# Mixtures of experts: rows gathered as quarters and transposed by VectorE, in place of whole rows and TensorE's transposes

## What is computed

```python
def hier_moe(x, norm_g, w_rg, w_re, w_gate, w_up, w_down):
    u = rms_norm(x, norm_g)
    lg = jnp.einsum('ntd,dg->ntg', u, w_rg)                 # 4 groups
    p_top, g_sel = lax.top_k(jax.nn.softmax(lg), 1)         # one group
    ...
    top_v, top_i = lax.top_k(le, TOP_K)                     # two of its 4 experts
    ...
    h = jax.nn.silu(jnp.einsum('ntd,edf->ntef', u, w_gate)) * jnp.einsum('ntd,edf->ntef', u, w_up)
    h = h * dense_w[..., None]
    return jnp.einsum('ntef,efd->ntd', h, w_down)
```

## Time and profile before

| | |
|---|---|
| median of 3 runs | 1412.71 us (1411.58 to 1415.81) |
| the profiled execution | 1418.34 us, its span 1416.5 us |
| TensorE busy | 1312.3 us, 93% of the span, mean granted clock 0.943 |
| VectorE, ScalarE, GpSimd busy | 38%, 21%, 12% |
| DMA | 437.02 MB, 309 GB/s mean; about 390 GB/s in the mixtures |

### The profile page before, as it was taken

How to read it: one execution, slowest core, us unless ns; L and a number is a source line. 1 busy time by engine, 2 the same in 40 slices (tenths; PEclk the granted TensorE clock), 3 DMA queues, 4 the chain that set the end, 5 groups by cost and what they waited for, 6 DMA issues and landing times.

```text
span 1416.5 us, 36477 instructions
## 1 busy us (share of the span) xinstructions
PE 1312.3 (93%) x15444; PEld 1004.0 (71%) x15444; DVE 540.7 (38%) x1274; ACT 297.5 (21%) x715; POOL 168.4 (12%) x202
## 2 busy tenths in 40 slices
PE   6979999999897989999989999999999799999996
PEld 5869999998535767666755655655546799999983
DVE  3740000000375647564756676664025200000005
ACT  2201111111231131313234343434110111111110
POOL 3110000010201111121211111120000100000003
PEclk9979999999997999999989899898998899999998
DMA  8959999998998699999978797974373599999976
GB/s 284 374 194 354 388 390 390 390 389 340 341 357 273 199 330 335 300 358 301 358 245 299 240 335 236 344 250 169 117 282 134 201 380 385 390 389 391 392 305 208
DMA packets 147223, 437.02 MB, mean 309 GB/s; under 512 B 20711, under 2 KB 51304, under 8 KB 138270
## 3 DMA queue, kind: packets, MB, share of 16 engines
q1 hardware_dynamic: 99494, 367.57, 70.1%
q10 hardware_dynamic: 37296, 38.09, 8.4%
q0 software_dynamic: 10320, 29.79, 6.7%
HBM read 406.31 MB, written 29.44 MB: 308 GB/s over the span
## 4 chain that ended last, share of the span: by engine, by line
PE 65%; issue 12%; DVE 9%; DMA 6%; ACT 3%; SPq 3%; ACTq 1%; POOL 1%; DVEq 0%; POOLq 0%
PE PS L1098 12%; PE PS L1102 11%; PE PS L1351 9%; PE PS L1130 6%; PE PS L1135 5%; PE PS L1485 5%; PE PS L1020 3%; PE PS L1391 2%; PE PS L1429 2%; PE PS L1437 2%; PE PS L1449 2%; SPq L680 1%; DMA W<-in_cache_v 1%; DVE KV L2425 1%; DMA KV<-in_cache_k 1%
## 5 line engine op out<-in xcount | busy, mean ns | idle before, releaser
L1102 PE MATMUL PS<-W,KV 128*32 128x128 f32 x3072 | 344.2, 274 | 0.0
L1098 PE MATMUL PS<-W,KV 128*32 128x384 f32 x3072 | 340.9, 490 | 3.2 <-DVE KV L2046 3.2
L1102 PEld LDWEIGHTS PS<-W,KV 128*32 128x32 f32 x3072 | 336.9, 111 | 1.9
L2286 DVE TENSOR_TENSOR KV<-KV,PS 128x384 f32<-128x384 f32 x32 | 17.7, 554 | 481.5 <-PE PS L1116 426.7
L1351 PE MATMUL PS<-W 128*128 128x256 f32 x768 | 178.2, 386 | 1.3 <-ACT KV L1758 1.3
L1351 PEld LDWEIGHTS PS<-W 128*128 128x128 f32 x768 | 144.2, 193 | 30.8 <-issue 8.8
L1130 PE MATMUL PS<-W,KV 128*32 128x384 f32 x1440 | 162.2, 489 | 0.0
L1135 PE MATMUL PS<-W,KV 128*32 128x256 f32 x960 | 162.2, 327 | 0.0
L2425 DVE STREAM_TRANSPOSE KV<-KV 128x1024 f32<-128x1024 f32 x128 | 154.9, 1226 | 7.8 <-DMA KV<-in_cache_k 7.7
L1098 PEld LDWEIGHTS PS<-W,KV 128*32 128x32 f32 x3072 | 150.5, 109 | 4.5 <-DVE KV L2046 4.1
L1135 PEld LDWEIGHTS PS<-W,KV 128*32 128x32 f32 x960 | 95.6, 109 | 14.4
(11 more groups left out here) (306 smaller groups left out, 1512.4 us busy)
## 6 DMA issues: line engine op xcount, KB each, us to landing
W<-in_w_gate SPq DMA_DIRECT2D x32, 2048.0 KB, 14.4
W<-in_w_up SPq DMA_DIRECT2D x32, 2048.0 KB, 15.5
W<-in_w_down SPq DMA_DIRECT2D x32, 2048.0 KB, 14.4
KV<-in_cache_k SPq DMA_DIRECT2D x256, 256.0 KB, 5.4
W<-in_cache_v SPq DMA_DIRECT2D x128, 512.0 KB, 7.7
yd<-KV ACTq DMA_DIRECT2D x30, 288.0 KB, 7.8
W<-in_w_kvf SPq DMA_DIRECT2D x4, 2048.0 KB, 18.2
W<-in_w_kvf ACTq DMA_DIRECT2D x8, 1024.0 KB, 8.6
```

Source lines behind the costliest of these rows:

```text
L1098: pe.matmul(PS[32 * q:32 * q + 32, bank, 0:WIDE], x, w[:, k, 0:WIDE], start=(k == 0), stop=(k == KC - 1), tile_position=(0, 32 * q), skip_ ...
L1102: mm = pe.matmul(PS[CAP:P, bank, P * q:P * q + P], x, w[:, k, WIDE:FF], start=(k == 0 and q == 0), stop=(k == KC - 1), tile_position=(0, C ...
```

## The change

A gathered row becomes four quarters of 256 features: XS is seen as `XS4`, in which row r is rows 4r to 4r + 3. XS is written with its features in another order (`in_quarters`), so that block transposes of 32x32 of a gathered tile give what the products need. Partition 32a + i of gather q holds quarter a of the expert's row 32q + i; three gathers of 128 quarters (1 KB each) make an expert. IDX is then a table of 3 columns for each expert, with 4 * row + a, written by 12 instructions in place of one. VectorE transposes the tile (one instruction) and multiplies it with the gains (three), into XQ[j], of which there are two, one in V4. TensorE's `x_tr` is gone; `up` gets a wait for `h_ready`, which `xt_ready` implied before.

```diff
@@ gather
-                        after(pool, sem("xt_tr"), e - 1 + l * NE)
+                        after(pool, sem("xg_read"), e - 1 + l * NE)
                         settled(pool)
-                        pool.indirect_dma_start(out=XG[j][0:CAP, :], out_offset=None, in_=XS,
-                                                in_offset=bass.IndirectOffsetOnAxis(ap=IDX[0:CAP, e:e + 1], axis=0))\
-                            .then_inc(sem(f"xg_in_{j}"), 16)
+                        for q in range(Q4):
+                            pool.indirect_dma_start(out=XG[j][:, 2 * P * q:2 * P * q + 2 * P], out_offset=None, in_=XS4,
+                                                    in_offset=bass.IndirectOffsetOnAxis(ap=IDX[:, Q4 * e + q:Q4 * e + q + 1], axis=0))\
+                                .then_inc(sem(f"xg_in_{j}"), 16)
@@ TensorE
-                def x_tr(e, j):
...
-                    transposes(XG[j], 0, CAP, KC).then_inc(sem("xt_tr"), 1)
...
-                            x = XT[:, k, 32 * q:32 * q + 32]
+                            x = XTQ[j][:, q, k, :]
...
                     else:
-                        product(3, 3 * j + 1, count, "up")
+                        after(pe, sem("h_ready"), e + l * NE)
+                        product(3, 3 * j + 1, count, "up", j)
...
                     if not first:
                         h_tr(e - 1)
-                    x_tr(e + 1, 1 - j)
-                    if not first:
                         down(e - 1, 1 - j)
...
-                x_tr(0, 0)
                 expert(0, 0)
@@ VectorE
+            def in_quarters(t, out):
+
+                r = ROWS[t]
+                return dve.tensor_scalar(out[0:r, :].rearrange("p (a k n) -> p a k n", a=4, k=KC),
+                                         H[0:r, t, :].rearrange("p (a n k) -> p a k n", a=4, k=KC), rs[0:r, t:t + 1], None, ALU.mult)
...
-                dve.tensor_copy(IDX[:, :], PS[:, 7, 2 * P:2 * P + NE]).then_inc(sem("routed"), 1)
+                table = IDX[:, :].rearrange("p (e q) -> p q e", q=Q4)
+                for q in range(Q4):
+                    for a in range(4):
+                        ins = dve.tensor_scalar(table[32 * a:32 * a + 32, q], PS[32 * q:32 * q + 32, 7, 2 * P:2 * P + NE], 4.0, float(a),
+                                                ALU.mult, ALU.add)
+                ins.then_inc(sem("routed"), 1)
...
-                def xt(e):
-                    dve.wait_ge(sem("xt_tr"), e + 1 + l * NE)
-                    gained(XT, 0, l, CAP).then_inc(sem("xt_ready"), 1)
+                def xt(e, j):
+                    dve.wait_ge(sem(f"xg_in_{j}"), 24 * e + 48 - 24 * j + l * (24 * NE))
+                    after(dve, sem("up_done"), e - 1 + l * NE)
+                    dve.transpose(XQ[j], XG[j][:, 0:Q4 * 2 * P]).then_inc(sem("xg_read"), 1)
+                    dve.wait_ge(sem("xg_read"), e + 1 + l * NE)
+                    x = XQ[j].rearrange("p (q k n) -> p q k n", q=Q4, k=KC)
+                    for q in range(Q4):
+                        g = gains[:, l, :].rearrange("p (k a) -> p k a", a=1).to_broadcast([P, KC, 32])
+                        ins = dve.tensor_tensor(x[:, q], x[:, q], g, ALU.mult)
+                    ins.then_inc(sem("xt_ready"), 1)
...
-                xt(0)
+                xt(0, 0)
+                xt(1, 1)
                 gates(l)
                 hidden(0)
-                xt(1)
+                xt(2, 0)
...
-                with dve.Fori(1, NE - 1) as e:
-                    hidden(e)
-                    xt(e + 1)
+                with dve.Fori(1, NE - 3, 2) as e:
+                    for j in range(2):
+                        hidden(e + j)
+                        xt(e + j + 2, 1 - j)
```

More of the change, by code:

```diff
@@ L340, in build @@
         SGi = sb("SGi", [P, 2, NT], I32)
[L341 to L342 removed]
+        IDX = sb("IDX", [P, NE * Q4], I32)
+        idc = sb("idc", [P, 2 * Q4], I32)
         npi = sb("npi", [1, 1], I32)
@@ L375, in build @@
         XT = V8[:, 4, :].rearrange("p (k n) -> p k n", k=KC)
+        XQ = [a[:, 0:Q4 * 2 * P] for a in (V8[:, 4, :], V4[:, :])]
+        XTQ = [a.rearrange("p (q k n) -> p q k n", q=Q4, k=KC) for a in XQ]
         SG = V8[:, 5, 0:FF]
@@ L1084, in moe, with product @@
             def moe(l):
-                def x_tr(e, j):
-                    k = 8 * e + 16 - 8 * j
-                    pe.wait_ge(sem(f"xg_in_{j}"), k + l * (8 * NE))
-                    after(pe, sem("xt_ready"), e + l * NE)
-                    transposes(XG[j], 0, CAP, KC).then_inc(sem("xt_tr"), 1)
-                def product(bank, slot, count, name):
+                def product(bank, slot, count, name, j):
                     pe.wait_ge(sem(f"w_in_{slot}"), count + l * (8 * NE))
@@ L1145, in halves @@
                         after(pe, sem("silu_done"), e + l * NE)
-                        product(2, 3 * j, count, "gate")
+                        product(2, 3 * j, count, "gate", j)
                     else:
-                        product(3, 3 * j + 1, count, "up")
+                        after(pe, sem("h_ready"), e + l * NE)
+                        product(3, 3 * j + 1, count, "up", j)
                 def expert(e, j):
@@ L1203, in moe @@
                             pe.wait_ge(sem(f"g_xg{l}"), 16 * (n + 1))
-                            transposes(XG[0], 0, P, KC).then_inc(sem(f"g_step{l}"), 1)
+                            for k in range(KC):
+                                for a in range(4):
+                                    at = 2 * P * a + 32 * k
+                                    mm = pe.matmul(PS[32 * a:32 * a + 32, k // 4, (k % 4) * P:(k % 4) * P + P], XG[0][:, at:at + 32], ident,
+                                                   start=True, stop=True, tile_position=(0, 32 * a), skip_group_check=True)
+                            mm.then_inc(sem(f"g_step{l}"), 1)
                             pe.wait_ge(sem(f"g_step{l}"), 9 * n + 2)
@@ L2024, in norm @@
                 norm_scale(phase, t)
+                if phase in ("r0", "r1"):
+                    return in_quarters(t, out)
                 if gain is None:
```

20 lines of the change are left out of this document (12 added, 8 removed).

## The result

The changed kernel takes 1434.51 us (median of 4 runs, 1432.71 to 1437.8), the kernel before 1413.78 (4 runs): the ratio is 1.0171, with a 95% interval of 1.0141 to 1.0202. It is slower by 1.7%, where I forecast 1408. The profiled span is 1436.0 us, 19.5 more than before.

What follows compares the result with a forecast made beforehand. TensorE was taken to set the pace, running on prefetched weights. The terms -11.5 - 3.2 - 1.0 + 2.0 + 5.2 + 1.3 + 2.5 gave -4.7 us, from 1412.7 to 1408.0 us, range 1400 to 1418.

Steps and rivals of the forecast that it cites:

- Part 1: TensorE between h_tr and down: each x_tr removed saves 0.41 us, not 1.06; 28 places, -11.5 us.
- Costed at nothing: In the loop, VectorE's 2.2 us and three gathers' 3.9 us of GpSimd for an expert lie beside TensorE; no cost.
- the weights come late: Rival: in the loops, smaller gather packets load the DMA and weight loads delay TensorE; 1423 at 86 ns a packet; chance 0.18.
- the DMA's own pace: Weight loads in the loop: the DMA wants about 18.2 us for an expert, TensorE 17.62, running on prefetched weights.
- Part 2: Between experts 0 and 1, x_tr(1) and its gains go from the path: 1.6 us in each layer, -3.2 us.
- the half clock: At gate(0), without x_tr, 1.3 more slow us in each layer, half lost: +1.3 us, bounds 0 and 2.7.
- Part 3: Mixture start, table to gate(0): table +2.0, gathers +5.2, VectorE's transposes and gains -1.0, slow clock +1.3 us.
- Part 4: Scalings that write rows in another order: +0.5 us for each of five on the path, +2.5 us (0 to 5).
- strided reads are slow: Rival: scalings at the skill's price for strided sources, or twice the upper bound; total 1415; chance 0.14.

Runs made afterwards that it cites:

- e5: The changed kernel with each expert's three gathers put apart, the later two behind the signals for down and gate, table used in place: 1416.94 us, ratio 1.004.
- e14: As e13, with the table given to GpSimd in three parts, so the first gather is issued after four of twelve instructions: 1384.13 us, ratio 0.9806.
- e13: The changed kernel with h_tr(e - 1) ahead of up(e), gathers paced apart, table in place, VectorE's copies for h_tr(0) before waiting for expert 2's rows: 1392.72 us.
- e2: The changed kernel with an expert's gathers waiting until the next down is done, so issued under the gate product, table in place: 1456.81 us, ratio 1.0326.
- e3: The changed kernel with h_tr(e - 1) ahead of up(e), gathers keeping their place: 1411.88 us, ratio 0.9997.
- e4: The kernel before with its one gather for an expert put off by about 3.2 us of idle elementwise work on GpSimd: 1411.5 us, ratio 1.0009.
- e7: The changed kernel with two gathers right behind each other and the third behind the signal that gate is done, table in place: 1427.1 us, ratio 1.0124.
- e1: The changed kernel with gathers issued earlier: table used in place, VectorE transposes the rows before it makes HH: 1435.28 us, ratio 1.0156.
- e16b: The changed kernel with a fourth gather of the same size for each expert, right behind the three: 1487.82 us, ratio 1.0552.
- e15b: The kernel before with five small plain DMAs from GpSimd behind each gather: 1412.62 us, ratio 1.0011.

## Why the prediction was wrong, by its steps

- **Part 1** (-11.5): the saving of 0.41 us at each place came exactly, 17.61 to 17.20 us, where no gather is issued. One thing was missed: in the loop every second down idles 0.85 us and not 0.58 (above, 320.63), though ScalarE's copy lasts as long; I take it for the waits against registers, which x_tr had covered; no run shows it. e5, free of stops, took 241.60 and 241.66 us for the loops against 245.33 and 245.31: -7.4 for 26 places, 3.3 less than forecast.
- **"Costed at nothing"** is the step that failed: "Three gathers take GpSimd 3.9 us of 17.6." I priced them on GpSimd's queue and in the DMA, and took TensorE for untouched since it neither waits for them nor shares an instruction with them. What the runs showed in its place: three issues in a row cost TensorE 0.9 us for each of the 22 experts that gather in the loops. They cost the loops 251.35 + 251.44 - 241.60 - 241.66 = 19.5 us. Of the rivals none had it; "the weights come late" had the right sign with the wrong mechanism, and its packets of 1 KB don't appear in the trace. The one after has 576 packets on the gathers' queue for the four experts in 250 to 320 us, 384 of 4 KB and 192 of 4 bytes: 96 of 4 KB for an expert, as before, and at 5.7% of the engines' time where the earlier trace rows have 6.5%. The 18.2 us that I had for the DMA's own pace don't hold either. In e14, at 16.5 us for an expert, the up loads from 148.2 to 297.0 land later by (15.4 - 11.1) / 9 = 0.48 us each, which by the same reckoning makes 17.0 us.
- **Part 2 and the half clock**: -1.9 with two of the 28 places -2.7; measured +3.6 (1.15 + 2.45). The half clock lasts 3.7 us of gate(0) in layer 0 (91.78 to 95.5), not longer than before, and 5.1 in layer 1 (1121.24 to 1126.3), 2.3 longer: with half of that lost about 1.2 us in all, near the 1.3 that I had. What is left, some 6.4 us against the forecast, stands where twelve gathers, for experts 0 to 3, are issued nearly in a row; in e13, with room between the gathers and h_tr ahead of up, the stretch is 24.7 and 24.1 us.
- **Part 3**: the table's instructions are 0.19 us apart and not 0.09, 2.05 us in all from 81.11 to 83.16 on the chain of waits; the third gather is issued 2.62 us behind the first (2.6 forecast); landing took 2.72 us and not 4.13, where I took the gain as nothing; VectorE's part 2.2, as forecast. gate(0) of layer 0 came 4.45 us late, 5.1 forecast (1.0 + 2.6 - 0.5, and 2.0 of part 4): the table 1.05 more, the landing 1.4 less and the scalings 0.3 less, misses that in good part cancel by luck.

```profile
83.16 0.19 DVE IDX L2206
...
84.21 1.02 POOL KV L847
...
86.83 2.72 DMA KV<-xs,IDX
...
89.57 0.99 DVE KV L2294
...
90.58 1.15 DVE KV L2299 x3
```

- **Part 4**: the view of the line of `in_quarters` gives a median of 1.15 us, 0.40 more than before (0.5 forecast). The rival "strided reads are slow" fell:

```profile
L2025 DVE TENSOR_SCALAR KQ<-H,rs x6: 1139/1151/1647, 32.5 to 1105.5; 128x1024 f32<-128x1024 f32 x4, 64x1024 f32<-64x1024 f32 x2
```

  That is 1.12 ns a column with a source that steps by 8 words. The 2.50 ns that I took from the Trainium skill, "Vector Engine (DVE) Microarchitecture Reference", section 5.2, is measured there with both sources of an instruction, or its destination, stepping by 24 words. This scaling has one source that steps and a contiguous destination, and this trace shows nothing of that price.

In all: loops 19.5 + 3.3, gate(0) to down(0) 6.3, less 3.8 at the two ways to gate(0) and 1.2 at the end, is 24.1 of the 24.2 us between the forecast of the span (-4.7) and what it did (+19.5). The stretches make up the span, so that this sum closes proves nothing by itself. Shown by experiments are the loops' 19.5 us (e5); of the 3.8, 3.1 lie on the way to gate(0) of layer 1, behind a stretch that differs by more than that between profiles.

## What to carry to other kernels

An engine that only issues transfers can stop one that never waits for it: look for gaps with the reason "issue" on the bound engine, and hold their times against the other queues. Where a loop has stretches with and without a suspect (here its last experts, beside which nothing is gathered), compare them before making any kernel. Gathers by index on GpSimd are best put one at a time between the products of TensorE; and when a covering step goes, move another product over the copy that it covered (h_tr ahead of up), which turned 0.41 us for an expert into 1.1.

## What the runs showed of the hardware

- While GpSimd issues gathers by index in a row, TensorE goes on for some 2.2 us (e2) to 3 us (e3, the kernel after) and then stops, with short pieces of work between, until 0.7 to 1.2 us behind the last issue. One gather at a time cost nothing in any expert of the loops (kernel before, e4, e5), a pair costs 0.4 to 0.5 us (e7), three 0.4 (e1) to 1.6 (e2), four 2.3 (e16b). A gather and five plain DMAs, 3.5 us of issues from the same queue, do not do it (e15b), nor 3.2 us of elementwise work (e4).
- Signals of TensorE are late in that time too: up to 2.1 us in e3. ScalarE's own work did not stop: in e2 y takes 0.81 us as everywhere, and its two stores are issued at 263.40 and 263.88, while a gather is issued from 263.01 on. That is the first of three, so it says little of the whole stop.
- What is held in TensorE's supply, and whether the reserve counts instructions or time, stays open: that its instructions are what is late is read from gaps with the reason "issue" and not from a view of the supply itself. e2 lost more (1.6 us) with its gathers under the gate product than the kernel after (0.9) with them under down, and a gate product has 96 matrix instructions in 5.2 us, down 80 in 5.1; that speaks for instructions, and is not shown.
